# Encoder with expert-choice mixture of experts on one core: hidden activations of experts 1 to 14 turned by VectorE in 32x32 blocks that DMA carries between partitions, and the rows' norm weight applied by ScalarE

## The reference

```
aff = softmax(xf @ router_w)                 # (512, 16)
gate, idx = top_k(aff.T, 64)                 # each expert picks 64 tokens
xs = xf[idx]                                 # (16, 64, 1024)
hid = silu(xs @ w_gate) * (xs @ w_up)        # (16, 64, 2048)
out = (hid @ w_down) * gate
y = zeros.at[idx].add(out)
```

## Time and profile before

| | us |
|---|---|
| median of three runs | 1548.18 (1548.04 to 1549.12) |
| the profiled execution | 1548.32 |
| its span, first to last instruction | 1546.5 |
| TensorE busy | 1535.3 (99%) |
| VectorE busy | 1310.5 (85%) |
| ScalarE busy | 1043.1 (67%) |
| GpSimd busy | 223.1 (14%) |
| one turn of the experts' loop | 66.66 |
| mean granted clock of TensorE | 0.999 of full |

### The profile page before, as it was taken

How to read it: one execution, slowest core, us unless ns; L and a number is a source line. 1 busy time by engine, 2 the same in 40 slices (tenths; PEclk the granted TensorE clock), 3 DMA queues, 4 the chain that set the end, 5 groups by cost and what they waited for, 6 DMA issues and landing times.

```text
span 1546.5 us, 22686 instructions
## 1 busy us (share of the span) xinstructions
PE 1535.3 (99%) x8378; PEld 1241.3 (80%) x8378; DVE 1310.5 (85%) x1386; ACT 1043.1 (67%) x985; POOL 223.1 (14%) x140
## 2 busy tenths in 40 slices
PE   9999999999999999999999999999999999999998
PEld 7888888888873888888888888888888888888886
DVE  7684786685766899999999999999999999999987
ACT  6453556343453777777777777777777777777777
POOL 0000001000022222120212202022120302210003
PEclk9999999999999999999999999999999999999999
DMA  9543438333466999999999999999999999999998
GB/s 343 188 139 115 154 137 280 102 123 99 146 238 233 397 420 403 402 401 382 413 380 393 393 386 415 376 406 386 395 402 369 417 382 405 388 386 408 363 393 340
DMA packets 156407, 498.60 MB, mean 322 GB/s; under 512 B 10880, under 2 KB 36608, under 8 KB 156352
## 3 DMA queue, kind: packets, MB, share of 16 engines
q1 hardware_dynamic: 144624, 461.54, 77.0%
q0 software_dynamic: 9280, 31.07, 6.5%
q10 hardware_dynamic: 2448, 5.25, 1.3%
HBM read 473.70 MB, written 20.97 MB: 320 GB/s over the span
## 4 chain that ended last, share of the span: by engine, by line
PE 96%; DMA 1%; ACT 1%; DVE 1%; SPq 0%; issue 0%; POOLq 0%; POOL 0%; DVEq 0%; ACTq 0%
PE ps L1974 82%; PE ps L2022 4%; PE ps L2113 2%; PE ps L2029 2%; PE ps L2071 2%; PE ps L2082 1%; PE ps L2430 1%; PE ps L2279 1%; DMA u_rows<-arena 1%; DMA raw<-w_qkv 1%; PE ps L2567 0%; PE ps L2275 0%; PE ps L2297 0%; DMA xh<-u_rows,first_rows_at 0%; SPq L588 0%
## 5 line engine op out<-in xcount | busy, mean ns | idle before, releaser
L1311 DVE TENSOR_TENSOR w_rest<-raw,w_high 128x2048 fp32r<-128x2048 f32 x212 | 506.9, 2402 | 65.8 <-ACT w_high L1188 48.3
L1188 ACT CAST w_high<-raw 128x2048 fp32r<-128x2048 f32 x184 | 352.5, 1916 | 139.5 <-PE ps L1974 139.4
L1974 PE MATMUL ps<-w_high,xt_high 128*128 128x512 f32 x984 | 304.8, 390 | 0.0
L1974 PE MATMUL ps<-w_rest,xt_high 128*128 128x512 f32 x984 | 304.6, 389 | 0.0
L1974 PE MATMUL ps<-w_high,xt_rest 128*128 128x512 f32 x984 | 304.5, 389 | 0.0
L1974 PEld LDWEIGHTS ps<-w_high,xt_high 128*128 128x128 f32 x984 | 184.7, 188 | 39.0 <-issue 0.8
L1311 DVE TENSOR_TENSOR w_rest<-early,w_high 128x2048 fp32r<-128x2048 f32 x90 | 206.7, 2299 | 10.7 <-ACT w_high L1188 10.7
L1974 PEld LDWEIGHTS ps<-w_high,xt_rest 128*128 128x128 f32 x984 | 184.8, 188 | 38.3
L1974 PEld LDWEIGHTS ps<-w_rest,xt_high 128*128 128x128 f32 x984 | 184.8, 188 | 38.3
L1311 DVE TENSOR_TENSOR w_rest<-raw_more,w_high 128x2048 fp32r<-128x2048 f32 x92 | 206.6, 2283 | 6.1 <-ACT w_high L1188 6.1
L1188 ACT CAST w_high<-early 128x2048 fp32r<-128x2048 f32 x90 | 172.3, 1915 | 58.1 <-PE ps L1974 58.1
(11 more groups left out here) (310 smaller groups left out, 2211.8 us busy)
## 6 DMA issues: line engine op xcount, KB each, us to landing
raw<-w_down SPq DMA_DIRECT2D x64, 1024.0 KB, 8.3
raw<-w_gate SPq DMA_DIRECT2D x62, 1024.0 KB, 8.4
raw<-w_up SPq DMA_DIRECT2D x62, 1024.0 KB, 8.1
raw_more<-w_down SPq DMA_DIRECT2D x32, 1024.0 KB, 8.4
early<-w_down SPq DMA_DIRECT2D x32, 1024.0 KB, 8.9
raw_more<-w_gate SPq DMA_DIRECT2D x31, 1024.0 KB, 9.0
raw_more<-w_up SPq DMA_DIRECT2D x31, 1024.0 KB, 8.8
early<-w_gate SPq DMA_DIRECT2D x31, 1024.0 KB, 9.0
```

What stands on the lines that cost most here:

```text
L1188: nc.scalar.copy(w_high[:, i % SLOTS, :], src).then_inc(high_done, 1)
L1311: nc.vector.tensor_tensor(w_rest[:, j, :], src, w_high[:, j, :].bitcast(F32), ALU.subtract).then_inc(rest_done, 1)
L1974: done = nc.tensor.matmul(out, lhs, rhs, start=start and part == 0, stop=stop and part == 2)
```

## The change

For experts 1 to 14 TensorE no longer turns the hidden activations. VectorE transposes each half in 32x32 blocks into `blocks` (`turn_hidden`). ScalarE then issues 16 DMAs (`move`), each of which carries 32 partitions x 256 columns (1 KB per partition) from partition group a of `blocks` to partition group c of `shuffled`, for all a and c. ScalarE copies the high part from there (`moved_high`), VectorE makes the rest (`moved_rest`). The rows of w_down are reordered on the host for these experts, so that the order of hidden columns that comes out is the right one. The move of the first half stands on ScalarE's stream after cast 21, that of the second half after cast 31 and the copy of the first half's high part; the second half's high part and rest are made in the next turn of the loop.

The norm weight is no longer multiplied in by GpSimd ahead of the transpose. The transposed rows have features on partitions, so ScalarE scales them in eight instructions of 128 x 128 with one weight per partition (`weigh_rows`, into `weighted_rows`), after cast 25. VectorE's row transpose waits for the gather itself. The weight comes in one 128 x 8 DMA instead of four broadcast ones.

The second half's gate product goes to banks 6 and 7 and its up product to 0 and 1, and TensorE's waits follow from that. Expert 0 and expert 15 are turned by TensorE as before.

```diff
+MOVES = QUARTERS * QUARTERS
...
+        def chunks(buf):
+            return buf[:, :].rearrange("p (k a n) -> p k a n", k=KC, a=QUARTERS)
+        def from_shuffled(h):
+            return arena[:, 2 + h, :].rearrange("p (a k n) -> p k a n", a=QUARTERS, k=KC)
...
-        piece_g = grow[:, 0:SPAN]
+        piece_g = mx[:, :, :].rearrange("p a i -> p (a i)")
+        weighted_rows = h_more[:, 0, :]
...
+        blocks = arena[:, 0:2, :]
+        shuffled = arena[:, 2:4, :]
...
-                    pool.wait_ge(rows_turned, e)
+                    pool.wait_ge(turned_step, rows_turned(e))
                 gather(e + 1)
-
-                pool.wait_ge(gathered, 16 + 16 * QUARTERS * (e + 1))
-                tokens = xg.rearrange("p (t n) -> p t n", t=QUARTERS)
-                weights = piece_g.rearrange("p (t n) -> p t n", t=1).broadcast_to([P, QUARTERS, SPAN])
-                nc.gpsimd.tensor_tensor(tokens, tokens, weights, ALU.mult).then_inc(rows_scaled, 1)
...
-                act.wait_ge(rows_turned, e)
-                nc.scalar.copy(xt_high[:, :], turned_rows).then_inc(xth_done, 1)
+                act.wait_ge(rows_scaled, KC * e)
+                nc.scalar.copy(xt_high[:, :], weighted_rows).then_inc(xth_done, 1)
+            def weigh_rows(e):
+                if isinstance(e, int) and e == 1:
+                    act.wait_ge(grow_in, 16 * 2)
+                act.wait_ge(turned_step, rows_turned(e))
+                act.wait_ge(xtr_done, e + 1)
+                for k in range(KC):
+                    at = slice(k * P, (k + 1) * P)
+                    nc.scalar.activation(weighted_rows[:, at], turned_rows[:, at], ACT.Copy, scale=piece_g[:, k:k + 1]).then_inc(rows_scaled, 1)
...
+            def move(e, h):
+                act.wait_ge(turned_step, hid_turned(e, h))
+                act.wait_ge(htr_done, 2 * e + h - 1)
+                for a in range(QUARTERS):
+                    for c in range(QUARTERS):
+                        tokens = blocks[a * QUARTER:(a + 1) * QUARTER, h, c * SPAN:(c + 1) * SPAN]
+                        place = shuffled[c * QUARTER:(c + 1) * QUARTER, h, a * SPAN:(a + 1) * SPAN]
+                        act.dma_start(place, tokens).then_inc(hid_moved, 16)
+            def moved_high(e, h):
+                act.wait_ge(hid_moved, 16 * MOVES * (2 * e + h - 1))
+                nc.scalar.copy(chunks(ht[h][0]), from_shuffled(h)).then_inc(hth_done, 1)
...
             with act.Fori(1, E - 2) as f:
-                highs(f, 12, 19)
+                highs(f, 12, 13)
+                moved_high(f, 1)
+                highs(f, 13, 19)
                 step_silu(2 * f + 2, pairs_before(f) + 16, 0)
-                highs(f, 19, 28)
-                step_silu(2 * f + 3, pairs_before(f) + 25, 1)
-                highs(f, 28, 31)
+                highs(f, 19, 22)
+                move(f + 1, 0)
+                highs(f, 22, 26)
+                weigh_rows(f + 2)
+                highs(f, 26, 28)
+                step_silu(2 * f + 3, pairs_before(f) + 25, 1, 6)
+                highs(f, 28, 30)
                 rows_high(f + 2)
-                highs(f, 31, 32)
-                hidden_high(2 * f + 2, 0, 2)
+                highs(f, 30, 32)
+                moved_high(f + 1, 0)
+                move(f + 1, 1)
                 highs(f, 32, 36)
-                hidden_high(2 * f + 3, 1, 6, pairs_before(f) + 32)
                 result(f, pairs_before(f) + 32)
...
-                nc.vector.tensor_tensor(acts[odd], bank(2, 2), acts[odd], ALU.mult).then_inc(hid_done, 1)
+                nc.vector.tensor_tensor(acts[odd], bank(up_bank, 2), acts[odd], ALU.mult).then_inc(hid_done, 1)
...
-                dve.wait_ge(rows_scaled, e)
-                nc.vector.transpose(turned_rows, xg.rearrange("p (t k n) -> p k t n", t=QUARTERS, k=KC)).then_inc(rows_turned, 1)
+                dve.wait_ge(gathered, 16 + 16 * QUARTERS * e)
+                if not (isinstance(e, int) and e == 1):
+                    dve.wait_ge(rows_scaled, KC * (e - 1))
+                nc.vector.transpose(turned_rows, xg.rearrange("p (t k n) -> p k t n", t=QUARTERS, k=KC)).then_inc(turned_step, 1)
...
+            def turn_hidden(e, h):
+                if not (isinstance(e, int) and e == 1):
+                    dve.wait_ge(hid_moved, 16 * MOVES * (2 * e + h - 3))
+                dve.wait_ge(hid_done, 2 * e + h + 1)
+                nc.vector.transpose(blocks[:, h, :], acts[h]).then_inc(turned_step, 1)
+            def moved_rest(e, h):
+                dve.wait_ge(hth_done, 2 * e + h + 1)
+                nc.vector.tensor_tensor(chunks(ht[h][1]), from_shuffled(h), chunks(ht[h][0]).bitcast(F32), ALU.subtract).then_inc(htr_done, 1)
...
             with dve.Fori(1, E - 2) as f:
-                rests(f, 12, 19)
+                rests(f, 12, 14)
+                moved_rest(f, 1)
+                rests(f, 14, 19)
                 step_hidden(2 * f + 2, 0)
+                rests(f, 19, 20)
+                turn_hidden(f + 1, 0)
+                rests(f, 20, 23)
                 turn_rows(f + 2)
-                rests(f, 19, 28)
-                step_hidden(2 * f + 3, 1)
-                rests(f, 28, 31)
+                rests(f, 23, 28)
+                step_hidden(2 * f + 3, 1, 0)
+                rests(f, 28, 29)
+                turn_hidden(f + 1, 1)
+                rests(f, 29, 31)
                 rows_rest(f + 2)
-                rests(f, 31, 32)
-                hidden_rest(2 * f + 2, 0, 2)
-                rests(f, 32, 36)
-                hidden_rest(2 * f + 3, 1)
-            rests(E - 2, 12, 20)
+                rests(f, 31, 34)
+                moved_rest(f + 1, 0)
+                rests(f, 34, 36)
...
-            def all_turns(e):
-
-                pe.wait_ge(hid_done, 2 * e + 2)
-                pe.wait_ge(htr_done, 2 * e)
-                if not isinstance(e, int):
-                    pe.nop(nofuse=True)
-                hidden_t(acts[0], 2)
-                hidden_t(acts[1], 6)
...
             with pe.Fori(1, E - 2) as f:
-                gate_up(f, 8, (xtr_done, f + 3), (htr_done, 2 * f + 1))
+                pe.wait_ge(hid_done, 2 * f + 2)
+                gate_up(f, 8, (0, 2), (xtr_done, f + 3))
                 pe.wait_ge(ys_done, f + 1)
                 down(2 * f, 0, f, 16, 0, 1)
-                gate_up(f, 17, (silu_done, 2 * f + 3), (hid_done, 2 * f + 3))
+                gate_up(f, 17, (6, 0), (silu_done, 2 * f + 2), (silu_done, 2 * f + 3))
                 down(2 * f, 0, f, 24, 1, 4)
-                all_turns(f + 1)
                 down(2 * f + 1, 1, f, 28)
```

More of the change, by code:

```diff
@@ L359, in encoder_kernel @@
         rows_scaled = sem("rows_scaled")
[L360 removed]
+        turned_step = sem("turned_step")
         uth_done = sem("uth_done")
@@ L450, in body_turn, with rows_turned, hid_turned @@
             return GU_PAIRS // RAW_SLOTS + (2 * (GU_PAIRS + D_PAIRS) // RAW_SLOTS) * e + i // RAW_SLOTS
+        def rows_turned(e):
+            return 1 if isinstance(e, int) and e == 1 else 3 * e - 3
+        def hid_turned(e, h):
+            return 3 * e - 1 + 2 * h
         def pairs_before(e):
@@ L736, in _ @@
                     nc.gpsimd.tensor_tensor(early_rows, early_rows, grow[0:CAP, :], ALU.mult).then_inc(early_scaled, 1)
[L737 to L740, removed]
+                    pool.wait_ge(nmx_done, HEADS * TRUNKS)
+                    pool.dma_start(piece_g, g_ffn_pieces).then_inc(grow_in, 16)
                 for k in full:
@@ L807, in _ @@
             scatter(E - 2)
-            pool.wait_ge(rows_scaled, E - 1)
+            pool.wait_ge(early_scaled, 1)
+            pool.wait_ge(grow_in, 16 * 2)
             load_grow(g_fin)
@@ L1148, in step_silu @@
                     return
-                nc.scalar.activation(acts[odd], bank(0, 2), ACT.Silu).then_inc(silu_done, 1)
+                nc.scalar.activation(acts[odd], bank(gate_bank, 2), ACT.Silu).then_inc(silu_done, 1)
             def rows_high(e):
@@ L1200, in _ @@
             highs(0, 5, 6)
-            act.wait_ge(early_done, 1)
+            act.wait_ge(early_mm, 2)
             act.wait_ge(h_out, 16 * TILES * TRUNKS)
@@ L1219, in _ @@
             act.wait_ge(gate_done, TRUNKS)
+            weigh_rows(1)
             rows_high(1)
@@ L2392, in _ @@
                 _, last = early_gate_up(kc)
-            last.then_inc(early_done, 1)
+            last.then_inc(early_mm, 1)
             def early_third(lo, hi):
@@ L2437, in places, with gate_up @@
                 nc.tensor.matmul(pieces, same_lane[:, :], spread_rows[:, :, :].rearrange("p t n -> p (t n)"), start=True, stop=True).then_inc(route_mm, 1)
-            def gate_up(e, lo, *banks_free):
+            def gate_up(e, lo, banks, *banks_free):
                 for i in range(GU_PAIRS):
@@ L2447, in gate_up @@
                         at = slice(kc * P, (kc + 1) * P)
-                        last = products([(bank(2 * (i % 2) + n), xt_high[:, at], xt_rest[:, at], *w(j, k * HALF + n * BANK, BANK),
```

(8 more changed lines are left out.)

74 lines of the change are left out of this document (42 added, 32 removed).

## The result

The changed kernel takes 1715.47 us (median of 4 runs, 1714.49 to 1716.12), the kernel before 1548.38 in the same rounds; the ratio is 1.1079, 95% interval 1.1065 to 1.1093. The forecast was slower, 1594, with 1538 to 1629 as range. The sign was right; the time lies beyond the range and even beyond rival 2's 1697.

A forecast was written before the change was run, and what follows sets the result against it. TensorE, busy 99% of the span, was taken to bound the kernel at 66.66 us per expert; 65.36 + 1.6 + 0.6 + 2.3 = 69.9, 3.25 more, times 14 is 45.5 on 1548.3: 1594 us, range 1538 to 1629.

The forecast's parts named there:

- rival 2: Moves on ScalarE: each issue costs 0.65 us, as in the only SBUF-to-SBUF row; +10.6 us per expert, 1697; chance 0.06.
- Turns gone, 1.3 us each, 65.36 left: TensorE, experts' loop: dropping 32 turning products saves 1.3 us per expert, leaving 65.36; 18.2 us over 14 experts.
- VectorE covered, with the 1.9 us lost beside GpSimd given back: VectorE, per expert: two more transposes of 1.16 us, less the 1.9 lost beside GpSimd's multiply; 62.0 of 65.36.
- TensorE's new waits and banks nothing; scalings 0.3 each and covered: Second half's products in other banks cost TensorE nothing; ScalarE's eight new scalings, 2.4 us per expert, fit its spare time.
- The moves, q = 0.42 per issue: ScalarE's 16 DMAs per move: each issue with its hand-over takes 0.42 us, between 0.365 and 0.475.
- the 0.62 row: Profile row of SBUF-to-SBUF issues in a row on ScalarE, 0.62 us each, 0.65 apart; its pattern has more dimensions.
- Stalls 16q - 5.1, + 0.6, 16q - 4.4: TensorE per expert: 1.6 us behind the first move, 0.6 for rest 23's lateness, 2.3 behind the second.
- DMA needs 66.0 to 67.5 per expert and does not bind: DMA per expert: 63.5 us plus 2.5 to 4.0 for the moves, more than TensorE's 65.36 but below 69.9.
- Rival 3's sub-case: DMA binds because 32-partition reads crowd: moves 6 us, 69.5 per expert, 1579 in all; rival's chance 0.08 overall.
- The two passages of the Trainium skill: On the moves' DMAs: dispatch about 50 ns, 0.8 us per 16 issues; small SBUF-to-SBUF pieces unpenalised, 2.5 us for the moves.

The follow-up runs named there:

- experiment 1: Changed kernel without any of the moves' DMAs; transposes, scalings, copies and banks stay: 1529.18 us.
- experiment 4: Changed kernel with the first half's 16 DMAs reading DRAM, the second half's copying 128 partitions of 256 B within SBUF: 1666.07 us.
- experiment 2: Changed kernel with each move's 16 issues spread on ScalarE, two behind each of eight casts: 1590.74 us, ratio 1.0275.
- experiment 3: Changed kernel with both moves issued in a row by SyncE instead of ScalarE: 1622.18 us.
- experiment 5: Changed kernel with all issues kept on ScalarE, each carrying 4 bytes per row in place of 1 KB: 1717.0 us.
- experiment 6: Changed kernel with four transfers per move in place of 16, each reading 32 partitions of 4 KB and writing all 128: 1547.95 us, ratio 0.9996.
- experiment 7: Kernel with four transfers per half, each copying 128 partitions of 1 KB to the same partitions: 1549.5 us.
- experiment 9: Kernel with four transfers per half, each now reading all 128 partitions and writing only 32: 1634.0 us.

## Why the prediction was wrong, step by step

It was 121 us too low. The rests of TensorE account for half: 8.8 us a turn where the sum had 1.6 + 0.6 + 2.3 = 4.5, 14 x 4.3 = 60 us. The half clock behind them, which no step had, is the other half, 57 us.

- *Turns gone, 1.3 us each, 65.36 left*: right (65.30, experiment 1).
- *VectorE covered, with the 1.9 us lost beside GpSimd given back*: right, 62.52 busy and single rests 2.28.
- *TensorE's new waits and banks nothing; scalings 0.3 each and covered*: right. All eight take 2.45 us in ScalarE's timeline; experiment 1 shows them free.
- *The moves, q = 0.42 per issue*: **the step that failed**, a mis-sized term in a right mechanism. Measured 0.64 with the hand-over. I had weighed the 0.62 row as an outlier (a pattern with more dimensions) against two rows of loads from DRAM. Experiment 4 shows that it was the only row of the right kind.
- *Stalls 16q - 5.1, + 0.6, 16q - 4.4*: at q = 0.64 they give 5.7 (with the 0.6) and 5.8 where the trace has 4.71 and 4.09. The 0.6 isn't there: no third rest is listed. The second is too large by 1.7: the issues start 0.24 us after cast 31 does and not with the copy, 1.6 us sooner than the formula has them. (10.9 - 6.4 is also 4.5 and not 4.4.) The rests together are 3 us smaller than the formula has them.
- *What no step had* (a second failed step: a term put at nothing): TensorE at half clock for 4.8 and some 3.4 us behind the two rests, 4.1 us a turn, 14 x 4.1 = 57 us. Loops with rests of 2.0 us at most (experiments 2 and 3) keep the mean at 0.997. This term lifts the time above rival 2's. Rival 2 had the right price of an issue, and that its 1697 came near is partly luck: rests 3 us a turn too long made up for most of the 4.1 that it lacked.
- *DMA needs 66.0 to 67.5 per expert and does not bind*: right that it doesn't bind in the changed kernel (experiment 5: without the bytes the same time), wrong in size for these pieces, 69.2 in experiment 2. The moves' 2.5 to 4.0 us hold for pieces that write all partitions: 66.2 in experiment 6, of which 2.9 are the moves' own packets (1024 of 46 ns over 16 engines); that leaves 63.3 for the rest, where the prediction had 63.5. Rival 3's sub-case had 6 us for crowding, 69.5 in all, and by reads; the size is near, and it is writes that crowd (experiments 6, 7 and 9).
- *The two passages of the Trainium skill* (DMA: Bandwidth & Descriptors). A dispatch of about 50 ns (section Anatomy of one DMA) stands in a table for the GpSimd path; it isn't the price of the issues here, by ScalarE and SyncE, which take 0.44 us from DRAM, nine times as much, and 0.61 from SBUF, twelve times. That copies within SBUF pay no penalty for small pieces (section Why small descriptors are slow) is nearly borne out by 1 KB pieces, 46 ns or 22 GB/s per engine beside 4 KB in 159 ns or 26; for 256 B in 18 ns, 14 GB/s, it isn't. What cost DMA most, 32 partitions as target, is no matter of the pieces' size.

The gain of 19 us is thus real. Against it stand, in the changed kernel, 8.8 us of rest and 4.1 of half clock per turn, both from 32 issues of 0.64 us in a queue with casts of weights behind them. With the issues spread DMA's price comes up, 3.9 us a turn above TensorE's 65.3. Of it 3.0 go when each move is four transfers that write all partitions (69.2 to 66.2), and 2.1 go already when only the shape changes and the 32 transfers stay (67.1).

Open: why writes to 32 partitions slow other queues' packets, and why the weights' packets stay at 173 to 180 ns in some stretches where no move is under way (1036 to 1038 us in spread, 1000 to 1010 in the kernel of experiment 9). Why an issue from SBUF takes longer than one from DRAM wasn't tried. Nor do these runs say how long a rest may be before the clock falls: 1.9 to 2.1 us left it alone 14 times in experiment 4, and 1.84 and 2.01 didn't in experiment 3.

## What to carry to other kernels

Price a new DMA by the row whose source memory is the same, and multiply by the number of issues before the bytes: 16 issues from SBUF are 10 us of an engine's queue, so look for a partition order, fixed on the host, that lets one transfer do the work of four. Let transfers write all 128 partitions. When a tuned kernel gets a wait of several microseconds on TensorE, add the half clock behind it (here 4.1 us to 8.8 of rest), and when two engines stand within 3% of each other, moving work from one to the other pays only up to the point where they meet: half of it here.

## What was unexpected of the hardware

- An issue's duration goes by its source: 0.443 us from DRAM and 0.61 to 0.63 from SBUF, in a row, on ScalarE; 0.59 on SyncE from SBUF. 4 bytes or 1 KB per row, 32 or 128 partitions make less than 0.02 us of difference.
- Four transfers that write 32 partitions each take DMA as a whole from 422 to 286 GB/s; four that read 32 and write 128 leave 415 of 421.
- ScalarE's sequencer runs ahead: in the second move the issues start at 1047.58, 0.24 us after cast 31 and 1.57 before the copy that stands ahead of them in the program.
- TensorE rested 4.71 us and went on at clock 0.5 for some 3.4 us, and each of the kernel's 28 long rests has a stretch of half clock behind it; of the rests near 2 us, 14 in experiment 4 left the clock at full and 2 in experiment 3 didn't.
